# Two transformer blocks on one core: mixers in another order, and norms whose roots are taken on one column per token block

## The reference

```
h = x + 0.5 * swiglu(rms_norm(x))                    # norm 0, feed-forward 1 (2816 wide)
u = rms_norm(h) @ w_in                               # norm 1
h = h + concat(hgrn2(u), latent_attention(u)) @ w_out   # FIRST MIXER
h = h + 0.5 * swiglu(rms_norm(h))                    # norm 2, feed-forward 2
h = h + sigmoid(rms_norm(h) @ w_g) * (p @ w_p)       # norm 3
x = rms_norm(h)                                      # the "plain" norm
z = modulate(rmsnorm(x), c) @ w_in_2                 # norm 4
y = g_a * pool(z) + g_b * forgetting_attention(z)    # SECOND MIXER, 16 heads
x = x + gt * (y @ w_out_2)
x = x + gt2 * peer(modulate(rmsnorm(x)))             # norm 5; top-16 of 16384 experts, 8 heads
out = rmsnorm(x)
```

## Time and profile before

| | |
|---|---|
| time, median of 3 runs | 1596.62 us (1594.4 to 1597.06) |
| the profiled execution | 1596.27 us, of which the span of instructions is 1594.5 us |
| busy: PE, DVE, POOL, ACT | 1400.5, 1004.2, 710.3, 561.5 us |
| chain that ended last | PE 49%, DMA 27%, DVE 13%, ACT 4%, issue 4%, POOL 3% |
| mean granted TensorE clock | 0.963 of full speed |

### The profile page before, as it was taken

How to read it: one execution, slowest core, us unless ns; L and a number is a source line. 1 busy time by engine, 2 the same in 40 slices (tenths; PEclk the granted TensorE clock), 3 DMA queues, 4 the chain that set the end, 5 groups by cost and what they waited for, 6 DMA issues and landing times.

```text
span 1594.5 us, 21201 instructions
## 1 busy us (share of the span) xinstructions
PE 1400.5 (88%) x8086; PEld 1071.4 (67%) x8086; DVE 1004.2 (63%) x1792; ACT 561.5 (35%) x947; POOL 710.3 (45%) x443
## 2 busy tenths in 40 slices
PE   8999899998999999989999998777777876877776
PEld 8999899978999998889889883333333332333322
DVE  4887464555778534552543777777777777777654
ACT  4443355424444334554343542222222222222212
POOL 3443437402343534486575485444433443444440
PEclk9999899999999999999999998999998998989998
DMA  5776673303577653243333379999999999999994
GB/s 221 264 263 229 242 251 134 106 27 116 208 263 261 213 180 107 105 135 130 106 107 112 137 289 422 422 421 421 421 421 422 421 421 422 421 422 421 422 421 187
DMA packets 59782, 427.15 MB, mean 268 GB/s; under 512 B 6640, under 2 KB 6960, under 8 KB 8624
## 3 DMA queue, kind: packets, MB, share of 16 engines
q0 software_dynamic: 36864, 268.45, 40.6%
q1 hardware_dynamic: 22176, 156.38, 27.9%
q10 hardware_dynamic: 656, 1.18, 0.2%
HBM read 424.93 MB, written 1.05 MB: 267 GB/s over the span
## 4 chain that ended last, share of the span: by engine, by line
PE 49%; DMA 27%; DVE 13%; ACT 4%; issue 4%; POOL 3%; DVEq 0%; SPq 0%; ACTq 0%; POOLq 0%
DMA rows_x<-in_expert_uv,arena 26%; PE ps L443 8%; PE ps L448 8%; PE ps L444 8%; PE ps L883 5%; PE ps L886 4%; PE ps L520 2%; POOL wlo L326 2%; PE ps L521 2%; PE ps L522 2%; DMA ring<-in_w 1%; DVE arena L1366 1%; DVE arena L1696 1%; ACT whi L947 1%; DVE arena L1512 1%
## 5 line engine op out<-in xcount | busy, mean ns | idle before, releaser
L326 POOL TENSOR_TENSOR wlo<-ring,whi 128x1024 fp32r<-128x1024 f32 x162 | 407.7, 2526 | 497.1 <-ACT whi L947 496.6
L443 PE MATMUL ps<-nh,whi 128*128 128x256 f32 x1440 | 364.3, 290 | 11.3 <-ACT nh L961 6.8
L947 ACT ACTIVATE whi<-ring 128x1024 fp32r<-128x1024 f32 x236 | 244.3, 1055 | 340.2 <-PE ps L448 139.4
L444 PE MATMUL ps<-nh,wlo 128*128 128x256 f32 x1440 | 355.7, 283 | 0.0
L443 PEld LDWEIGHTS ps<-nh,whi 128*128 128x128 f32 x1440 | 276.4, 192 | 17.2 <-issue 8.1
L444 PEld LDWEIGHTS ps<-nh,wlo 128*128 128x128 f32 x1440 | 276.7, 192 | 0.3
L448 PE MATMUL ps<-nl,whi 128*128 128x256 f32 x1440 | 209.2, 285 | 0.1
L448 PEld LDWEIGHTS ps<-nl,whi 128*128 128x128 f32 x1440 | 188.2, 192 | 4.9 <-DVE nl L1304 2.1
L326 DVE TENSOR_TENSOR wlo<-ring,whi 128x1024 fp32r<-128x1024 f32 x74 | 103.8, 1414 | 133.8 <-ACT whi L947 128.6
L1844 POOL DMA_INDIRECT arena<-in_expert_uv,arena x96 | 111.3, 1160 | 141.0 <-PE ps L886 129.4
L1696 DVE CUSTOM_DVE_ANT_0 arena<-arena 128x1024 f32<-128x1024 f32 x96 | 124.7, 1299 | 39.7 <-DMA arena<-in_expert_uv,arena 35.6
(11 more groups left out here) (323 smaller groups left out, 2393.6 us busy)
## 6 DMA issues: line engine op xcount, KB each, us to landing
ring<-in_w SPq DMA_DIRECT2D x118, 1024.0 KB, 5.0
arena<-in_wmod SPq DMA_DIRECT2D x24, 1024.0 KB, 5.0
small<-in_small SPq DMA_DIRECT2D x2, 938.5 KB, 7.0
arena<-in_expert_uv,arena POOLq DMA_INDIRECT x96, 26.5
h<-in_x SPq DMA_DIRECT2D x2, 512.0 KB, 5.6
keys<-in_keys SPq DMA_DIRECT2D x1, 1024.0 KB, 7.0
rows_w<-in_expert_uv,arena POOLq DMA_INDIRECT x64, 25.0
small<-in_small SPq DMA_DIRECT2D x1, 939.0 KB, 6.8
```

Of the source, the lines that this page charges most:

```text
L326: return v.tensor_tensor(wlo[:, tile % TILES, :], ring[:, tile // 2 % RAW, at:at + TILE], whi[:, tile % TILES, :].bitcast(F32), ALU.subtract)
L443: mm(to, hi[:, k, :], nh[:, k, :], start=(k == 0), stop=False)
L444: mm(to, lo[:, k, :], nh[:, k, :], start=False, stop=False)
L947: fn(whi[:, tile % TILES, :], ring[:, slot % RAW, at:at + TILE], ACT.Copy).then_inc(S("high_w"), 1)
```

## The change

Five things are done. (1) The sums of squares are made the other way round: the squares are the stationary operand, ones the moving one, so that the sum stands with one token a partition, and one column for each block of 128 tokens holds all of it. Root and reciprocal work on 128x2 in place of 128x256. A new step, `spread`, multiplies the column, broadcast, with the identity, which puts the inverse roots on all partitions again, in PSUM, and `scaled` reads it there. The first sum of each norm starts with a product of zeros. (2) `load_root` puts a one-element root ahead of the last squares. (3) `keep_busy(15)` in the norms becomes 3 before and 3 after `spread`; all filler in the mixers goes. (4) In the first mixer the levels stand between half slots, and the silu gate slots go behind the scores. (5) In the second mixer half slots and pool products stand between the steps of the rounds; `g_b` comes before `g_a`, so that each group is gated as it comes; GpSimd converts tiles after two of its four pool additions in place of all four.

```diff
-                last = mm(ps[:, 4, 0:T], ones[:, :], sq[:, c, :], start=(c == 0), stop=(c == C - 1))
+                last = sums_of_tokens(4, sq, c)
+            def sums_of_tokens(bank, x, c):
+                if c == 0:
+                    mm(ps[:, bank, 0:T], zeros[:, :], ones[:, :].unsqueeze(1).to_broadcast([P, TB, P]), start=True,
+                       stop=False, skip_group_check=True)
+                for b in range(TB):
+                    last = mm(ps[:, bank, b * P:(b + 1) * P], x[:, c, b * P:(b + 1) * P], ones[:, :], start=False,
+                              stop=(c == C - 1), skip_group_check=True)
+                return last
+            def spread(m):
+                pe.wait_ge(S("root_inverted"), m + 1)
+                for b in range(TB):
+                    last = mm(ps[:, 4, T + b * P:T + (b + 1) * P], rinv[:, b:b + 1].to_broadcast([P, P]), ident,
+                              start=True, stop=True, skip_group_check=True)
+                last.then_inc(S("spread"), 1)
-                keep_busy(15, bank=6)
+                keep_busy(3, bank=6)
+                spread(m)
+                keep_busy(3, bank=6)
...
-                fn(std[:, 0, :], ps[:, 4, 0:T], ACT.Sqrt, bias=eps[:, 1:2] if m == 4 else eps[:, 0:1], scale=1.0 / D
+                fn(std[:, 0, 0:TB], ps[:, 4, 0:T:P], ACT.Sqrt, bias=eps[:, 1:2] if m == 4 else eps[:, 0:1], scale=1.0 / D
-                own(v.reciprocal(rstd[:, 0, :], std[:, 0, :]))
+                v.reciprocal(rinv[:, 0:TB], std[:, 0, 0:TB]).then_inc(S("root_inverted"), 1)
...
+            features(S_IN + 4, between=lambda: level(0, hq, hk))
             level(1, hqf, hk)
+            features(S_IN + 5, between=lambda: level(2, hqf, hk))
             level(3, hqf, hk)
+            tokens(S_IN + 6, between=sums_and_level)
+            latent_spread()
+            level(5, hqf, hk)
+            tokens(S_IN + 7, between=lambda: level(6, hqf, hk))
+            level(7, hqf, hk)
+            q_up(1)
+            q_up(2)
+            last_level()
+            q_up(3)
+            hg_out()
...
+            attention(0, mla_score)
+            pe.wait_ge(S("hg_scaled"), 1)
+            features(S_IN + 8)
+            features(S_IN + 9)
+            turn_probs(0, m["pr"])
+            values(0, mla_value)
...
+            features(slot + 6)
+            fa_turn(2)
+            features(slot + 7, halves=(0,))
+            fa_scores(3)
+            fa_values(2)
+            features(slot + 7, halves=(1,))
+            features(slot + 8, halves=(0,))
+            pool_product(0)
+            features(slot + 8, halves=(1,))
+            pool_product(1)
+            fa_turn(3)
...
+            for group in range(4):
                 softmax(n, s["pr"], s["st"], float(AD) ** -0.5)
+                if group:
+                    attended(group - 1)
                 normalise(n, s["pr"], s["st"])
+            pool_gated(0)
```

More of the change, by code:

```diff
@@ L467, in tokens @@
                         last = mm(to, nl[:, k, cols], hi[:, :, k, :], start=False, stop=(k == C - 1))
+                    if between and b == 0:
+                        between()
                 last.then_inc(S("tiles_done"), 2)
@@ L554, in residual @@
                 square_sum(m, C - 1)
+                keep_busy(3, bank=(slot + 2) % BANKS)
+                spread(m)
                 if plain:
@@ L591, in _ @@
             pe.wait_ge(S("con_landed"), 16)
-            keep_busy(12, bank=5)
+            keep_busy(3, bank=5)
+            spread(0)
+            keep_busy(3, bank=5)
             swiglu(S_FFN1, 0, 0, 1, 0)
@@ new lines, in hg_bank, with hg_sums, hg_spread @@
+            def hg_bank(at):
+                return ps[:, 2 + at // 4, at % 4 * P:(at % 4 + 1) * P]
+            def hg_sums():
+                pe.wait_ge(S("hg_squared"), 1)
+                for at in range(HH * TB):
+                    hd, b = at // TB, at % TB
+                    last = mm(hg_bank(at), osq[:, hd, b * P:(b + 1) * P], ones[:, :], start=True, stop=True)
+                last.then_inc(S("hg_sums"), 1)
+            def hg_spread():
+                pe.wait_ge(S("hg_inverted"), 1)
+                for at in range(HH * TB):
+                    last = mm(hg_bank(at), rsmall[:, 2 * TB + at:2 * TB + at + 1].to_broadcast([P, P]), ident,
+                              start=True, stop=True)
+                last.then_inc(S("hg_spread"), 1)
@@ new lines, in fa_scores, with fa_values, pool_product @@
+            def fa_scores(group):
+                attention(group + 1, fa_score(group))
+            def fa_values(group):
+                if group == 0:
+                    pe.wait_ge(S("banks_freed"), S_IN2 + 12)
+                values(group + 1, fa_value(group))
+            def pool_product(g):
+                if g == 0:
+                    pe.wait_ge(S("pooled"), 1)
+                    pe.wait_ge(S("attended_read"), 4)
+                elif g == 3:
+                    pe.wait_ge(S("probsT_copied"), 5)
+                else:
+                    pe.wait_ge(S("pool_read"), g)
+                for t in range(2):
+                    last = mm(ps[:, 5 if g == 3 else 4, t * T:(t + 1) * T], w_pool[:, g, t * P:(t + 1) * P],
+                              pooled[:, g, :], start=True, stop=True)
+                last.then_inc(S("pool_ready"), 1)
@@ new lines, in _ @@
+            fa_turn(2)
[8 more added lines that the diff above has]
+            fa_turn(3)
+            features(slot + 9, halves=(0,))
+            pool_product(2)
+            features(slot + 9, halves=(1,))
+            pool_product(3)
+            pe.wait_ge(S("pool_read"), 3)
```

356 lines of the change are left out of this document (201 added, 155 removed).

## The result

| | before | after |
|---|---|---|
| median, 15 runs of each in turn | 1596.61 us (1591.42 to 1606.18) | 1588.92 us (1583.50 to 1593.30) |
| ratio after / before | | 0.9947, 95% interval 0.9933 to 0.9961 |
| the profiled execution (span) | 1596.27 us (1594.5) | 1584.69 us (1582.9) |
| mean granted TensorE clock | 0.963 | 0.951 |

A forecast was written before the change was run, and what follows sets the result against it. Outside the DMA-bound experts, TensorE waits on VectorE and ScalarE chains. Norms 7.1, first mixer 4.3 and second 11.3, less 5.8 for the clock, give 16.9 us: 1596.27 to 1579.4 us, chance 0.45; 8-in-10 range 1565 to 1590.

The forecast's parts named there:

- the four waits of 3 us and more: One TensorE wait in the first mixer, three in the second; each charged 1.45 us for a clock fall, 5.8 us together.
- The ones of 2 us: TensorE's waits of about 2 us, left uncharged; the clock might fall at them or not.
- 2.1 us for the rotation: First mixer: TensorE's wait for the rotation, put at 2.1 us with no clock loss charged.
- the wait of 3.1: End of the first mixer: after the scores, two slots of 11.5 us do not cover softmax, exp and normalisation; TensorE waits.
- 2.85 were forecast as gain: First mixer: 4.3 us gained by the new order, with 1.45 us charged for the clock.
- 11.3 - 4.35: Second mixer: 107.7 us against 118.98, so 11.3 gained, with 4.35 charged for three falls of the clock.
- The norms: All norms: earlier root, shorter root and reciprocal, `spread` and a hidden table load save 7.1 us in sum.
- the one term that rested on an operand in PSUM not contending: Norm 0: `scaled` freed from GpSimd's conversions, four chunks in 1.64 us in place of 3.75; 2.4 us in all.
- Norm 4: Gains only 0.5 us: two sums open with zeros, and ScalarE does the plain norm's root before its first `nh`.
- The clock falls at each wait: Rival, chance 0.22: no filler left in the mixers, five more waits of about 2 us cost 1.45 each; 1586.6 us.
- the first rival: The waits shrink further, chance 0.25: normalisation meets no conversions and the exp's delay is hidden; 10 us more, 1569 us.
- The slower and the unchanged case: Slower, 0.04: ScalarE's list lengthens second-mixer rounds, 1603 us. No change, 0.04: weight stream takes the freed time back, 1596 us.

The follow-up runs named there:

- fill_rope: Changed kernel plus 8 filler products (1.9 us) in TensorE's wait for the rotation, just ahead of the first mixer's scores; 1577.91 us, 0.9893 of the kernel before.
- first_as_before: Changed kernel with the first mixer put back as before, large roots and 44 filler products included; 1578.01 us, 0.9897 of the kernel before.
- fill_first: Changed kernel with filler in all the longer waits of the first mixer, the rotation's included, none in the second; 1575.49 us, 0.9879 of the kernel before.
- norms_only: Kernel before with the new norms alone, both mixers as they were; 1589.12 us, 0.9950 of the kernel before.
- half_early: fill_rope with the first half of the last gate slot moved ahead of the second pool product in the second mixer; 1578.84 us, 0.9889 of the kernel before.
- second_as_before: Changed kernel with the second mixer put back as before, 12 filler products included; 1596.56 us, 1.0003 of the kernel before.
- fill_others: Changed kernel with filler in the first mixer's other waits, none in the wait for the rotation; 1586.05 us, 0.9941 of the kernel before.
- half_behind_wait: Changed kernel with the first half of gate slot S_IN + 8 between the rotation wait and the scores, roots in other PSUM banks; 1588.83 us, 0.9963 of before.
- exp_first: fill_rope with the second mixer's exps of groups 1 and 3 ahead of the gate sigmoids on ScalarE; 1578.73 us, 0.9885 of the kernel before.

## Why the prediction was wrong, and where it was right

**The step that failed** is the clock in the first mixer. The prediction put it as "I charge the four waits of 3 us and more: 3.1, 3.0, 4.5, 6.0", with 1.45 each, and "The ones of 2 us lie between the two rows and could go either way". The price came from sixteen score records of the second mixer, which take 4.33 instead of 2.88. In the first mixer the wait that cost the clock was the forecast's own 2.1 us for the rotation, which it had left uncharged, and the price was not 1.45; the wait of 3.1 that it did charge came out at 1.22 and cost no clock. From the windows: the scores 14.24 - 8.35 = 5.9, the gate slot's 3.84 us at 0.50, 1.9; another fall of 3.4 us behind the wait for level 0, 1.7; less 2.82 - 1.22 = 1.6, which the slow scores took from the next wait. That is 7.9, and the filled kernel's first mixer is 136.91 - 129.40 = 7.5 us shorter; by the ratios the filler is worth 8.6. What I had not asked is how long the lower level lasts: the earlier trace rows holds one fall, of 3.4 us, and I took its price for the price of any. The trace that I forecast from already held another, the 10.24 us at 0.50 behind the wait of 3.50 us in feed-forward 1.

By the ratios the first mixer lost about 8.2 us where 2.85 were forecast as gain, 11 us of difference; norms and second mixer gave 2.6 more than forecast, and so the whole misses by 8.5. The 8.2 and the clock's 8.6 are differences of ratios, good to 4 or 5 us; in the two profiled executions the first mixer's own stage differs by 4.3. Of the 11, the clock has 8.6 - 1.45 = 7. The rest is the order itself: with filler it beats the old first mixer by 0.6 us (fill_rope against first_as_before) to 2.9 (fill_first), by its own stage in the profiles by 132.57 - 129.40 = 3.2, and I had 4.3.

**The waits were right.** I forecast waits of 1.95, 1.3, 0.5, 2.2, 2.0, 0.8, 2.1 and 3.1 us for the first mixer. The changed kernel has 1.82, 0.90, none, 1.92, 1.69, 0.78, 2.14 and 1.22, and with the clock kept the last is 2.82. The filled first mixer took 129.40 us, against 128.3 forecast without the clock. In the second mixer 3.0, 4.5, 2.4 and 6.0 were forecast and 3.04, 4.60, 1.14 and 6.18 measured. That stage gave 118.98 - 109.84 = 9.1 us where 11.3 - 4.35 = 6.95 was forecast: its falls of the clock, 3.4, 3.4 and 6.8 us long, cost partly time in which TensorE then waited anyway. Removing them by filler gave 4.7 us in the profile, and 0.9879 to 0.9862, 2.7 us, in time, which the intervals do not tell from nothing.

**The norms** gave 8.0 us by norms_only (4.8 to 11.2), forecast 7.1. Root, reciprocal and spread took 0.26, 0.17 and 0.71, forecast 0.3, 0.2 and 0.6. In norm 0 VectorE scales six chunks in 2.43 us beside a conversion of GpSimd from 17.76 to 20.22, 0.41 each; before, four took 3.75, of which the first, beside a conversion from 17.33 to 20.68, took 2.56. That is the one term that rested on an operand in PSUM not contending (the Trainium skill, SBUF — State Buffer, Who interferes with whom); the trace agrees. Norm 4 went the other way, +0.17 for -0.5: the time from its last sum to the next slot fell from 5.81 to 5.07 us, 0.7 where I had 1.4, and that last sum began 0.9 later in its stretch, with two products of zeros of 0.4 to 0.5 each and the early table load ahead of it. The missing 0.7 stands in VectorE's list:

```profile
646.86 2.92 DVE L1697 TENSOR_SCALAR coef<-mod 128x8 f32<-128x8 f32 x1
...
649.00 0.26 ACT L1027 ACTIVATE std<-ps,eps 128x2 f32<-128x2 f32 x1 [0.85 <-PE ps L495]
...
650.22 0.17 DVE L1396 RECIPROCAL rinv<-std 128x2 f32<-128x2 f32 x1
```

The root ended at 649.26, but the reciprocal stood behind three small operations on the modulation's coefficients and began 0.96 later, where in norm 1 it began 0.03 later. The first of the three took 2.92 us, and 1.44 in the kernel before.

**The rivals.** "The clock falls at each wait" was the nearest, at 1586.6, and its time is the one that came true, though not as written: not five more falls of 1.45, but one of them of 8. That its number lies 2.3 us from the measured 1588.92, and that the range of 1565 to 1590 holds it, is luck of sizes and not of mechanism. The Trainium skill's rule that half rate is the default and activity lifts it (TensorE: Matmul & The Clock Gate, Part 1: The HAM clock gate) does not by itself foretell what the scores did: TensorE was busy for all of their 14.24 us and stayed at half rate for most of them. I had used the rule to count falls and not to ask how one ends. The waits did not shrink as the first rival had it, but for 1.14 in place of 2.4 us in the third round. The slower and the unchanged case did not come, and the stage of the experts kept its length, 709.77 us against 710.23.

**What stays open.** The profiled execution is 11.6 us under that of before, the medians 7.7. Most of that gap is in feed-forward 1, where the clock was low for 10.2 us at 165.6 before and for 3.4 at 165.8 after, half of the difference being 3.4 us. Such a fall stands behind a wait for converted weights, and in the twelve profiles of the experiments it is 10.2 us long four times, 3.4 twice and absent six times: it goes with the execution, for of two kernels with the same code up to there fill_rope has none and half_early has 10.2. In feed-forward 2 the changed kernel waited 3.71 us for weights, with 3.4 us of lower clock. In the seven profiles whose first mixer kept its clock (fill_first's but for its first 1.6 us) that stretch is 207.5 to 214.0 us, mean 209.2; in the three that ran the scores at the lower clock throughout (the changed kernel, second_as_before, fill_others) it is 209.6 to 212.6, mean 211.3. That would be 2 us of what the ratios charge the first mixer beyond its own stage, but the spreads overlap, and no run isolates it. Nor was it tried why TensorE keeps its clock in some executions of one program and not in others.

## What to carry to other kernels

Filler that is removed has to be priced by the clock that it kept, and one fall is not the price of the next: look in the trace for every stretch at the lower level and how long it lasts, and ask of each wait that is left bare which products follow it, and for how long. In a chain of VectorE and ScalarE that sets the pace, work moved ahead of a wait is missing in the next one, so follow the order through to where the time comes out. And an operation of VectorE with two operands in SBUF that is moved earlier must be looked at anew beside GpSimd's.

## What the runs showed of the hardware

- Behind a wait of 2.14 us TensorE ran at 1.2 GHz in place of 2.4 for 17.1 us in the changed kernel, although it was busy without a gap all that time: the lower level lasted through the scores, of which half the products have 64 rows, and ended 3.8 us into the gate slot. In second_as_before and fill_others it lasted 20.5 us. With the gate slot's products directly behind the same wait it lasted 3.4 us (half_behind_wait, one profile).
- The clock can fall with no wait ahead: in exp_first and half_early it fell 3.2 us into the scores, for 13.7 us, and in exp_first TensorE was busy 7.50 of the 7.66 us ahead of that, with one pause of 0.16.
- Waits of one length differ: the 1.82 ahead of level 0 was followed by 3.4 us at the lower level in the changed kernel and by none in fill_rope, the 1.92 ahead of level 6 by none in either, but by 3.4 us in exp_first. And the length of the wait does not set that of the fall: 10.2 us beside a wait of 5.67 in half_behind_wait, 6.8 beside 6.18 in the second mixer, 10.2 beside 3.50 in the kernel before.
- One program varies with the clock from execution to execution: exp_first from 1572.40 us at a mean of 0.960 to 1589.90 at 0.946.
